# Two-layer model on one core: zero matmuls at the start of the first layer and in its mixer's rounds

## The reference

```
x = x + parallel_mixer(rms_norm(x, mix_norm_g), w_in, conv_w, conv_b, igate_b, fgate_b, ...)
x = x + memory_cross_attention(...)      # x attends to 256 memory tokens
x = x + peer_ffn(...)                    # experts gathered by index
# then second_block: gated delta rule, sliding-window attention, two conv FFNs
```

## Time and profile before

| | |
|---|---|
| median of 3 runs | 1861.38 us (1858.18 to 1863.12) |
| profiled execution, its own time | 1859.58 us |
| its span, first to last instruction | 1857.8 us |
| PE busy | 1615.4 us (87%) |
| DVE / ACT / POOL busy | 1207.9 / 832.1 / 376.2 us |
| mean granted TensorE clock | 0.949 of full |
| chain that ended last | PE 59%, DMA 17%, DVE 13%, ACT 8% |
| 75 to 218 us (the mixer's rounds and the pieces after them): PE busy | 122.82 of 143.00 us, clock 0.93 |

### The profile page before, as it was taken

The page is one execution under the profiler, slowest core; times in us unless marked ns, Lnnn a source line. Parts: engine busy times, 40 slices in busy tenths (PEclk is TensorE's granted clock), DMA queues, the critical chain, the costliest instruction groups (busy, mean ns, idle before and its releaser), DMA issues.

```text
span 1857.8 us, 24060 instructions
## 1 busy us (share of the span) xinstructions
PE 1615.4 (87%) x9314; PEld 1222.8 (66%) x9325; DVE 1207.9 (65%) x2395; ACT 832.1 (45%) x1703; POOL 376.2 (20%) x327
## 2 busy tenths in 40 slices
PE   7878989798977777888788888879999998999999
PEld 6768988555423333222244767769999876579999
DVE  5676566778787787455655666546775546557764
ACT  5645544453544344333534542235554425345542
POOL 1010012445434434434441002002000100010000
PEclk9989999899988988999999989989999999899999
DMA  6312443899999999999996311114444521025554
GB/s 252 137 68 91 161 180 114 326 396 426 426 416 400 390 391 377 426 428 426 428 425 266 114 68 46 46 47 180 167 167 160 188 91 59 11 91 182 182 169 150
DMA packets 63593, 421.15 MB, mean 227 GB/s; under 512 B 8180, under 2 KB 11512, under 8 KB 15608
## 3 DMA queue, kind: packets, MB, share of 16 engines
q0 software_dynamic: 36864, 268.45, 35.0%
q1 hardware_dynamic: 23952, 148.70, 22.5%
q10 hardware_dynamic: 2664, 2.47, 0.4%
HBM read 418.54 MB, written 1.05 MB: 226 GB/s over the span
## 4 chain that ended last, share of the span: by engine, by line
PE 59%; DMA 17%; DVE 13%; ACT 8%; issue 2%; POOL 0%; SPq 0%; ACTq 0%; DVEq 0%
PE bank L304 57%; DMA uv<-in_uv,idx 16%; DVE lows L367 3%; DVE uv L1353 2%; ACT L316 2%; DVE cacc L320 1%; PE bank L2446 1%; ACT dg L316 1%; PE bank L309 1%; DMA slabs<-in_w_in 1%; ACT acts L316 1%; ACT wp L312 1%; ACT wf L312 0%; DVE t L320 0%; POOL uv L1467 0%
## 5 line engine op out<-in xcount | busy, mean ns | idle before, releaser
L304 PE MATMUL bank<-uv,dg 128*128 128x512 f32 x1024 | 495.9, 629 | 121.7 <-ACT dg L316 121.6
L304 PEld LDWEIGHTS bank<-uv,dg 128*128 128x128 f32 x1024 | 192.5, 198 | 414.7 <-ACT dg L316 221.8
L1353 DVE CUSTOM_DVE_ANT_0 uv<-uv,htok 128x1024 f32<-128x1024 f32 x256 | 313.0, 1223 | 186.8 <-DMA uv<-in_uv,idx 185.5
L1467 POOL DMA_INDIRECT uv<-in_uv,idx x256 | 294.6, 1151 | 383.5 <-PE bank L304 327.5
L367 DVE TENSOR_TENSOR lows<-slabs,wp 128x2048 fp32r<-128x2048 f32 (+1 forms) x78 | 168.3, 2157 | 58.4 <-ACT wp L312 58.2
L304 PE MATMUL bank<-hn,lows 128*128 128x272 f32 (+2 forms) x704 | 200.9, 285 | 0.0
L482 POOL TENSOR_TENSOR sqT<-sqT 128x256 f32<-128x256 f32 (+1 forms) x42 | 51.4, 1225 | 692.9 <-ACT sqT L316 690.3
L312 ACT ACTIVATE wp<-slabs 128x2048 fp32r<-128x2048 f32 (+1 forms) x78 | 140.6, 1803 | 78.1 <-DMA slabs<-in_dn 30.4
L367 DVE TENSOR_TENSOR lows<-slabs,whl 128x2048 fp32r<-128x2048 f32 (+1 forms) x52 | 110.4, 2124 | 49.9 <-ACT whl L312 49.7
L316 ACT ACTIVATE acts<-acts 128x1 f32<-128x1 f32 x256 | 50.3, 196 | 195.1 <-DVE acts L1353 195.0
L304 PE MATMUL bank<-hh,lows 128*128 128x272 f32 x448 | 136.0, 304 | 0.0
(11 more groups left out here) (382 smaller groups left out, 3025.5 us busy)
## 6 DMA issues: line engine op xcount, KB each, us to landing
slabs<-in_up SPq DMA_DIRECT2D x44, 1024.0 KB, 4.8
slabs<-in_w_in SPq DMA_DIRECT2D x28, 1024.0 KB, 4.8
slabs<-in_dn SPq DMA_DIRECT2D x32, 704.0 KB, 4.1
slabs<-in_wkv SPq DMA_DIRECT2D x8, 1024.0 KB, 4.8
slabs<-in_w_out SPq DMA_DIRECT2D x8, 1024.0 KB, 4.8
slabs<-in_pq SPq DMA_DIRECT2D x8, 1024.0 KB, 4.8
slabs<-in_wq SPq DMA_DIRECT2D x4, 1024.0 KB, 4.8
slabs<-in_wo SPq DMA_DIRECT2D x4, 1024.0 KB, 4.8
```

The lines of the kernel that those rows point to most:

```text
L304: ins = T.e.matmul(pr[2] if len(pr) > 2 else out, pr[0], pr[1], start=(start and k == 0), stop=(stop and k == len(pairs) - 1), skip_group_ ...
L1353: V.e.tensor_tensor_reduce(u_, u_, htok[:, n, :], 1.0, 0.0, ALU.mult, ALU.add, acts[:, n, e_:e_ + 1]).then_inc(*V.up("dot", q))
L1467: G.e.indirect_dma_start(uv[q % NU][:, :], None, d["uv"][:, :], bass.IndirectOffsetOnAxis(ap=idx[:, n, e_:e_ + 1], axis=0)).then_inc(s_uv[ ...
```

## The change

GpSimd clears the first 128 columns of a mixer buffer (`t384[7]`, used otherwise by the stick-breaking heads) at its first instruction of the kernel, and TensorE waits for that and issues 40 bf16 matmuls on it (128 x 128 stationary, 256 columns moving) into the bank of the first piece. In `mixer_plan` a round without a piece, as long as pieces are left, gets an entry `idle` with the name of the next piece. TensorE issues 4 such matmuls there, into that next piece's bank, from the block of zeros in the mask `NMI`, after the wait for the evacuation that the piece itself would wait for. VectorE and ScalarE skip the entry. Nobody reads the results: the piece that follows starts its accumulation anew.

```diff
                 if n in places:
                     out.append(pieces.pop(0))
+                elif pieces:
+                    out.append(("idle",) + pieces[0][1:])
...
+        def zeros_tensor(name, i, j, zeros, count):
+            was = PBANK[name, i, j][1]
+            if was:
+                T.wait_ge(*evac_lane(*was).at("ev", *was))
+            for _ in range(count):
+                T.e.matmul(pbank(name, i, j)[:, 0:T1], zeros[:, 0:P], zeros[:, 0:T1], start=True, stop=True, skip_group_check=True)
+
         def mix1_tensor():
             T.stage("mix1")
+            T.wait_ge(*G.at("zeros"))
+            zeros_tensor("w_in", 0, 0, t384[7][:, 0:P].bitcast(BF16), 40)
...
+                elif x[0] == "idle":
+                    zeros_tensor(x[1], x[2], x[3], NMI[:, P:2 * P].bitcast(BF16), 4)
... (vector and scalar program: the entry is skipped)
         def mix1_gpsimd():
             G.stage("mix1")
+            G.e.memset(t384[7][:, 0:P], 0.0).then_inc(*G.up("zeros"))
```

More of the change, by code:

```diff
@@ L907, in mix1_vector @@
                     continue
+                if x[0] == "idle":
+                    continue
                 if x[0] == "ahead":
```

## The result

The changed kernel takes 1864.9 us (median of 20 runs, 1858.86 to 1870.91), the kernel before 1859.68 us (20 runs, 1851.97 to 1865.51). The ratio is 1.0032, 95% interval 1.0019 to 1.0044: slower by some 6 us, between 3.5 and 8. The forecast was 1862.4 us, +1.0 us. The range held the time; the size of the move was not foreseen. That the time came out only 2.5 us from the forecast is in part luck: the forecast was added to the median of the three runs known then, 1861.38 us, and that of 20 runs is 1.7 us lower.

A forecast was written before the change was run, and what follows sets the result against it. The chain was taken as a transfer up to about 24 us, then from 75 us TensorE alternating with VectorE and ScalarE. Start 0, batches +5.6, clock -4.6: +1.0 us on the median of 1861.38, 1862.4 us; range 1855.5 to 1868.

The forecast's parts named there:

- Part 2, the price of a batch: First mixer's rounds: each batch of four zero matmuls takes 0.47 us; 12 inside TensorE's chain stretches add 5.6 us.
- Rival B: Zero batches: each weight load adds its time, 0.86 us a batch, 1867.1 us in all; chance 0.05.
- Which batches are hidden: First mixer: 20 of 32 batches stand before a TensorE wait that takes them, so they cost nothing.
- Part 3, the clock: First mixer: shorter waits remove some falls to half clock at 89 to 178 us, -4.6 us (bounds 0 and -8.75).
- about 2.2 us or more mostly brings one fall: TensorE: an idle stretch of that length mostly brings 3.4 us at half clock; at 1.75 us it is open.
- Part 1, the start: Before the first piece: 40 zero matmuls end before it and count 0, bounds -1.7 and +1.7 us.
- A: First mixer: the clock still falls at each wait, leaving only the batches' +5.6 us, 1867.0 us; chance 0.14.
- C: First mixer: all five falls to half clock go, -3.1 us, 1858.2 us; chance 0.18.
- D: First mixer: VectorE takes up TensorE's gain, half of the 3.4 us at 123 and 133 us lost, 1864.1 us; chance 0.15.
- Later stages: After the first mixer: something unpriced, as falls of the clock come elsewhere; chance 0.05.

The follow-up runs named there:

- rounds only: Changed kernel without the 40 zero matmuls at the start, all 32 batches kept: 1858.20 us, ratio 1.0002 to the kernel before.
- hidden and two more: Changed kernel without start zeros and the 12 chain batches, plus 12 zero matmuls in each of two idle stretches before the rounds: 1851.30 us, ratio 0.9949 to before.
- before again: The kernel before, unchanged, timed as if it were a changed one: 1861.16 us, ratio 1.0006.
- start only: Changed kernel without zeros in the rounds, only the 40 at the start; timed twice: 1863.72 and 1864.14 us, ratios 1.0030 and 1.0016 to before.
- hidden batches only: Changed kernel with only the 20 batches before a TensorE wait, no start zeros and no chain batches: 1852.93 us, ratio 0.9974 to before.
- path batches only: Changed kernel with only the 12 batches inside TensorE's chain stretches, none before waits, no start zeros: 1861.76 us, ratio 1.0018 to before.

## Why the prediction was right or wrong

- *Part 2, the price of a batch:* right, 0.45 us where 0.47 was taken; the 12 batches in the chain take 5.8 us where 5.6 was counted. Of the changed kernel, a batch and what follows it:

```profile
143.91 0.60 PE L562 MATMUL bank<-con 128*128 128x256 bf16 x4
144.26 0.48 PE L304 MATMUL bank<-h,wf 128*128 128x256 f32 x2
```

 The next work starts 0.35 us after the batch. Over a whole stretch it is more: the one that began at 177.35 us and ended at 217.39 now runs from 179.57 to 220.61, 41.04 us instead of 40.04, and 1.7 us of a fall are gone, so six batches cost 2.7 us, 0.45 each. Rival B, with each load added, would have made it 0.86 us. The rule beside it (the Trainium skill, TensorE: Matmul & The Clock Gate, Part 3, "What overlaps and what doesn't") lets a weight load overlap matmuls in flight only where it addresses other rows of the array. This trace disagrees: each of these matmuls loads all 128 rows, and four of them with their loads take 0.45 us.
- *Which batches are hidden:* right. The 20 with the 12 left out gain 4.8 us by the ratio, where -4.6 us was counted for the falls; the 12 alone cost 3.4 us (0 to 6.7), where +5.6 was counted.
- *Part 3, the clock:* the falls at 123 and 133 us went, one of the two at 102.9 stayed, that at 89 went, all as taken or at the better end; that at 178 us went too in the profile of the changed kernel, with 2.08 us of idle time left, but stayed in that of rounds only with 2.10 us. So part of this agreement is luck. The rule "about 2.2 us or more mostly brings one fall" does not hold in either direction: idle stretches of 2.50 and 2.49 us (hidden and two more) and of 2.48 us (before again, at 137.57) brought none, and falls followed 1.55 us (start only, at 27.99) and 1.71 us (before again, at 26.61). It also had no place for the fall at 75 to 80 us, which comes without idle time and stands in 10 of 13 profiles. But kernels with and without zeros have that one, so nothing shows that it moves the difference. The +1.0 us forecast for the rounds agrees with rounds only (-0.2 us by the medians, up to 3.7 us over), whose interval is too wide to confirm it. One size was misread by a little: the work under the falls at 102.9 us is 4.5 us (105.28 to 109.8), not 4.3.
- *Part 1, the start:* this is the step that failed. "I count nothing of it" was argued from the first pieces, which are not in the chain; that holds, the first piece starts at 10.46 us and the fall is merely moved to 11.9. The bounds of -1.7 to +1.7 us thought only of the clock. TensorE's longer program was not counted as traffic, though the step began with the statement that the chain there is a transfer. The first 1.4 us are that. With the part that stays open the start makes about 5 us, 3 to 7, which is enough for the whole of the measured +5.2 us. The first piece of w_out was forecast 0 to 2 us later and is 3.2 us later: 1.4 from the start and 1.8 from the mixer.
- *Rivals:* A (1867.0, all falls stay) is not what happened, though its time is as near as the forecast's. C (no fall left) did not happen either. D is not needed: of the 3.4 us at 123 us and at 133 us nearly all came through (30.7 us between the steps at 121.62 and at 152.34 before and 28.9 us, with three batches in it, between 125.65 and 154.54 after: 30.7 - 3.4 + 1.4 + 0.2). A cost at the start was in none of the priced rivals.
- *Later stages:* from the first piece of w_out to the end the first profile of before takes 1639.0 us and the changed kernel's 1647.1, but hidden batches only 1639.8 and path batches only 1635.4. The kernel before again takes 1636.2 us there. Single executions scatter by so much that a difference of 5 us is hidden in any one profile.

## What to carry to other kernels

Zeros that keep TensorE's clock up paid here only where TensorE waits anyway. Put them directly before a wait and none into a stretch in which TensorE is the chain; filling the waits further brought nothing that these runs could tell. Here 20 batches of the 32 and 24 matmuls more give 8 us, all 32 give nothing. Instructions are traffic as well: where a kernel begins with transfers in the chain, a longer program for one engine can bring its next fetch into the middle of them. And where executions scatter by 16 us, a single profile shows where a fall stands in it, but not whether a change pays.

## What the runs showed of the hardware that was not expected

- The granted clock fell without idle time: in the changed kernel TensorE is busy 4.40 of 4.40 us at clock 1.00, half of it with matmuls of 4 rows, and then has 7 us at 0.52. Ten of 13 profiles have such a fall in that place. That the 4 rows are the reason is not shown.
- The length of an idle stretch does not decide whether the clock falls: 1.55 us was followed by a fall in one profile, 2.50 us by none in another.
- In the first 3.4 us of work of the kernel before the clock column says 1.00, while matmuls take 0.21 us. With zeros ahead the same pieces start at full pace (0.12 us each) and the fall at 11.9 us is in the record.
- An instruction fetch of 0.02 MB held one DMA engine for 1.1 us, and a 1 MB slab over all 16 landed 1.4 us later. With the fetch some 3 us behind the slab it was not late, and with the fetch near the slab's end it was 0.4 us late.
- Weight loads of all 128 rows overlap the matmuls in flight: 36 matmuls and 35 loads fill 4.00 us each in the same 4.00 us, and a batch of four zero matmuls with their loads costs 0.45 us.
- The same kernel spreads over 16 to 20 us (0.9 to 1.1%) between executions on one chip, and the places of the falls differ from one to the next.
